# Finishing tokens ahead of the last expert, and half of the first additions on GpSimd

## The chip, the cores and the metric

One core of a Trainium2 chip runs the program; float32 throughout. The time is device microseconds of one execution. Before the change three runs took 1734.29 to 1737.38 us, median 1736.76.

## The reference

One layer of a hybrid decoder on 1024 tokens of width 1024: RMSNorm, a combined projection, a linear-recurrence branch and an attention branch, merged, projected and added to x. Then, and here the change lies, RMSNorm, a mixture of 32 experts and a final RMSNorm:

```python
comb_w = p_group * jax.nn.softmax(top_v, axis=-1)      # a token has two experts, in one group of eight
hb = jax.nn.silu(xb @ w1[e]) * (xb @ w3[e])            # expert e on its tokens: 1024 -> 512
y = hb @ w2[e]                                         # 512 -> 1024
out = x + sum over the token's two experts of w * y
return rms_norm(out, g_final)
```

So a token is finished by: its x, plus low-numbered slot's row times its share, plus high-numbered slot's row times its share, squares summed, root, reciprocal, and the product with g_final.

## The kernel before, in words

Float32 products are made of three products of split operands: ScalarE makes a high part (`piece_hi`, L2032), VectorE the low part (`piece_lo`, L2038, two inputs in SBUF), TensorE multiplies (L2054 for gate and up, L2067 for down). The 1024 tokens are 8 tiles of 128 rows, the residual x2 stays in SBUF.

The last stage (`route_experts`, L2571) first routes (`rest`, L1767): per tile, the last product is added to x2 (`add_rows`), the row is normalized, stored to xn_d, and experts are chosen. Then `experts` (L2070) runs one body per expert. Each expert has 96 slots (BLK); slot rows are gathered from xn_d by an indirect DMA that POOL issues (L2122), one body ahead. Weights come in pieces of 1 MB, six per expert, into a ring of 12 buffers (e_raw), all issued by SP (L2022) in order; a piece waits until TensorE has used the one 12 pieces earlier. An expert's result leaves PSUM by a ScalarE copy (`rows_out`, L2196) and is stored to y_d (`rows_store`, L2200). An expert with more than 96 rows has its surplus in extra blocks behind the 32 (`beyond`, an If on a count from memory, with a loop).

Between the first six bodies VectorE does small chained operations on [128, 8] and [128, 32] tiles (`surplus`, `places`, `destinations`, `blocks`, `row_order`, `shares`, L2403 to L2453): where each token's rows lie and what shares they have. `Steps.did` makes each wait for the one before it. `row_order` stands between bodies 4 and 5, `shares` between 5 and 6.

The end, all programs in order on their engine: POOL, when expert 30's rows are stored, issues eight gathers `EARLY` (L2273) of each token's lower slot row, as far as it lies before expert 31, into tiles `near`, which lie over the piece buffers 0 to 3; a row that lies in expert 31 gets a zero share. VectorE adds each, times its share, to x2 (L2456). When expert 31's rows are stored, POOL issues eight gathers `LATER` of the higher slot row into tiles `far`, over buffers 4 to 7. Per tile VectorE adds, ScalarE squares and sums (L2393) and takes the root (L2395), VectorE takes the reciprocal (L2468) and multiplies (L2472), one and two tiles behind the add; SP stores the tile to out (L2250):

```python
            for t in range(NT):
                dve.wait_ge(near_added, t + 1)
                dve.wait_ge(far_in[t], 16)
                add(far, LATER, t, added)
                if t >= 2:
                    norm(t - 2)
                if t >= 1:
                    root(t - 1)
```

Of the kernel before, what the change touches and what calls it, by code (L numbers as in the profile page):

```python
# [108 lines left out]
class Kernel:  # L109
    def __init__(self, nc, ins, out):  # L110
# [13 lines left out]
        self.slots_d = dram("slots_d", (SLOTS + BLK, 1), I32)  # L124
        self.y_d = dram("y_d", (SLOTS, D))
# [1476 lines left out]
    def project_first(self):  # L1602
# [17 lines left out]
        self.rows_of = high.put("rows_of", [P, 3, NT], I32)  # L1620
        self.share = high.put("share", [P, 3, NT])
# [23 lines left out]
        prod, before_t = put("rt_prod", [P, NT, NE]), put("rt_before_t", [P, NT + 1, NE])  # L1645
        e_base = self.e_base = put("rt_ebase", [P, NT, NE])
# [120 lines left out]
        def rest():  # L1767
# [7 lines left out]
            to_exp, exped = sem("rt_to_exp"), sem("rt_exped")  # L1775

            def sync(sp):
# [246 lines left out]

    def piece_hi(self, act, piece):
# [44 lines left out]
    def experts(self):  # L2070
# [16 lines left out]
        swapped, kept, here, one, two, row = (order.put(f"ls_{n}", [P, NT]) for n in ("swapped", "kept", "here", "one", "two", "row"))  # L2087
# [3 lines left out]
        total, mean, rstd, power = (final.put(f"cb_{n}", [P, NT]) for n in ("total", "mean", "rstd", "power"))  # L2091
        small = final.put("cb_small", [P, 1])
        over = {"near": Map(nc, self.work_start, self.high), "far": Map(nc, self.act_start + 4 * NT * D, self.raw_end)}
        near, far = ([over[n].put(f"cb_{n}{t}", [P, D]) for t in range(NT)] for n in ("near", "far"))
        EARLY, LATER, SURPLUS = range(3)
# [6 lines left out]
        g_in, const, surplus_ready, near_added, surplus_added, added, squared, rooted, powered, normed, out_stored = (  # L2102
            sem("cb_" + n) for n in ("g", "const", "surplus_ready", "near_added", "surplus", "added", "squared", "rooted", "powered", "normed", "stored"))
        ROOT = D ** -0.5

# [119 lines left out]
        def sync(sp):  # L2225
# [21 lines left out]
            beyond(sp, other, before=lambda: sp.wait_ge(near_added, NT))  # L2247
            for t in range(NT):
                sp.wait_ge(normed, t + 1)
                sp.dma_start(k_.out[t * P:(t + 1) * P, :], far[t][:, :]).then_inc(out_stored, 16)  # L2250
            sp.wait_ge(out_stored, 16 * NT)

        def gpsimd(pool):

            for j in range(2, NE):
                gather(pool, j, j % 2, k_.slots_i[0:BLK, j:j + 1])
            pool.wait_ge(dest_out, 2)
# [10 lines left out]
            pool.memset(power[:, :], -0.5).then_inc(const, 1)  # L2268
            pool.memset(small[:, :], EPS).then_inc(const, 1)

            def rows(which, t, to, done):
                upto = BLK * (NE - 1) if which == EARLY else SLOTS
                pool.indirect_dma_start(out=to[t][:, :], out_offset=None, in_=k_.y_d[0:upto, :],  # L2273
                                        in_offset=bass.IndirectOffsetOnAxis(ap=k_.rows_of[:, which, t:t + 1], axis=0))\
                    .then_inc(done[t], 16)

            def all_stored(n):
                pool.wait_ge(y_stored[0], 16 * (NE // 2 + (n + 1) // 2))
                pool.wait_ge(y_stored[1], 16 * (NE // 2 + n // 2))

            def surplus_rows(n):
                pool.wait_ge(const, 2)
                pool.wait_ge(near_added, NT)
                all_stored(n)
                pool.tensor_tensor(total[:, :], power[:, :], power[:, :], ALU.mult).then_inc(surplus_ready, 1)
                pool.wait_ge(surplus_ready, 1)
                for t in range(NT):
                    rows(SURPLUS, t, near, near_in)
# [4 lines left out]
            for t in range(NT):  # L2293
                rows(EARLY, t, near, near_in)
# [102 lines left out]
        def vector(dve):  # L2397
# [125 lines left out]
            for t in range(NT):  # L2523
# [3 lines left out]
                if t >= 2:  # L2527
                    norm(t - 2)
# [68 lines left out]
```

## Time and profile before

| | us |
|---|---|
| three runs | 1734.29, 1736.76, 1737.38 |
| profiled execution, own time | 1740.18 |
| its span, first to last instruction | 1738.5 |
| TensorE busy | 1641.7 (94%) |
| VectorE busy | 1240.6 (71%) |
| ScalarE busy | 898.6 (52%) |
| POOL busy | 132.5 (8%) |

The span is what the trace covers; the profiled execution's own time is 1.7 us longer. A busy share is an average over stages: in the expert stage, from about 1123 us, TensorE and the DMA engines are both busy nearly all the time, in the last 38 us TensorE does nothing. Times inside the trace are from the span's start. DVE is VectorE, ACT ScalarE, POOL GpSimd; a q behind a name is the engine's instruction queue issuing a DMA.

### The profile page before, as it was taken

What the parts mean: (1) busy time and instruction counts of PE and PEld (TensorE: products, weight loads), DVE (VectorE), ACT (ScalarE), POOL (GpSimd) and SP (SyncE); (2) the same over time, 40 slices, a digit from 0 to 9 for tenths busy, and PEclk for the clock granted to TensorE, in tenths of its full rate; (3) what the DMA queues carried; (4) which work ended last, traced back from release to release, by engine and by line L of the source; (5) the groups of instructions that cost most, each with busy time, mean ns of one, the idle gap of its engine ahead of it and who ended that gap; (6) DMA issues with size and microseconds to landing.
All of it is one profiled execution on the core that took longest, in us unless ns stands there. A gap on an engine that the chain in (4) does not pass through costs nothing. (4 is left out here: it accounts for less than half of the span.)

```text
span 1738.5 us, 22942 instructions
## 1 busy us (share of the span) xinstructions
PE 1641.7 (94%) x8288; PEld 1312.9 (76%) x8288; DVE 1240.6 (71%) x1505; ACT 898.6 (52%) x1038; POOL 132.5 (8%) x180
## 2 busy tenths in 40 slices
PE   6999999999999999999989999699999999999991
PEld 6888888888888898778878898566677777777660
DVE  6877776666349882277764426699988888888886
ACT  6343343334237650166642112377777878787773
POOL 1000000000011100022200000100000000000104
PEclk9999999999999999999999999799999999999995
DMA  5354453333255442577662321599999999999988
GB/s 172 88 180 146 159 180 99 103 114 122 97 157 143 131 136 98 205 245 235 240 209 97 144 66 61 208 386 397 399 392 398 389 398 392 398 391 395 397 317 296
DMA packets 187095, 398.97 MB, mean 229 GB/s; under 512 B 16576, under 2 KB 96592, under 8 KB 186000
## 3 DMA queue, kind: packets, MB, share of 16 engines
q1 hardware_dynamic: 172464, 336.96, 53.7%
q0 software_dynamic: 8384, 29.63, 5.8%
q10 hardware_dynamic: 6176, 31.46, 4.8%
q8 instruction: 42, 0.69, 0.2%
q14 instruction: 29, 0.24, 0.0%
HBM read 326.35 MB, written 71.65 MB: 229 GB/s over the span
## 5 line engine op out<-in xcount | busy, mean ns | idle before, releaser
L2038 DVE TENSOR_TENSOR e_l<-e_raw,e_h 128x2048 fp32r<-128x2048 f32 x192 | 439.2, 2290 | 64.4 <-ACT e_h L2032 63.9
L2032 ACT ACTIVATE e_h<-e_raw 128x2048 fp32r<-128x2048 f32 x192 | 368.2, 1919 | 87.5 <-PE ps L2067 44.5
L2054 PE MATMUL ps<-e_h,e_xth 128*96 128x512 f32 x512 | 205.1, 401 | 5.1 <-DVE e_l L2038 3.2
L2054 PE MATMUL ps<-e_h,e_xtl 128*96 128x512 f32 x512 | 202.7, 396 | 0.0
L2054 PE MATMUL ps<-e_l,e_xth 128*96 128x512 f32 x512 | 201.8, 394 | 0.0
L823 DVE TENSOR_TENSOR wn_stl<-wn_stl,ps 128x512 f32<-128x512 f32 x140 | 96.0, 686 | 56.4 <-PE ps L771 49.3
L223 PE MATMUL ps<-uh,w_h 128*128 128x512 f32 x384 | 122.6, 394 | 6.8 <-DVE ul L1340 3.8
L223 PE MATMUL ps<-ul,w_h 128*128 128x512 f32 x384 | 122.2, 393 | 0.0
L223 PE MATMUL ps<-uh,w_l 128*128 128x512 f32 x384 | 122.0, 392 | 0.0
L2054 PEld LDWEIGHTS ps<-e_h,e_xth 128*96 128x96 f32 x512 | 83.0, 162 | 45.2 <-issue 7.4
L2054 PEld LDWEIGHTS ps<-e_h,e_xtl 128*96 128x96 f32 x512 | 83.0, 162 | 36.2
L2054 PEld LDWEIGHTS ps<-e_l,e_xth 128*96 128x96 f32 x512 | 83.4, 163 | 32.2
L795 ACT ACTIVATE wn_stl<-wn_stl 128x512 f32<-128x512 f32 x48 | 30.5, 635 | 133.2 <-DVE wn_stl L823 133.2
L223 PEld LDWEIGHTS ps<-uh,w_h 128*128 128x128 f32 x384 | 72.4, 189 | 23.1 <-DVE ul L1340 4.6
L2067 PE MATMUL ps<-e_h,e_hth 128*96 128x512 f32 x256 | 82.4, 403 | 2.4 <-DVE e_htl L2191 2.4
L223 PEld LDWEIGHTS ps<-ul,w_h 128*128 128x128 f32 x384 | 73.1, 190 | 15.3
L223 PEld LDWEIGHTS ps<-uh,w_l 128*128 128x128 f32 x384 | 72.8, 190 | 15.5
L2067 PE MATMUL ps<-e_l,e_hth 128*96 128x512 f32 x256 | 80.6, 396 | 0.0
L2067 PE MATMUL ps<-e_h,e_htl 128*96 128x512 f32 x256 | 80.3, 395 | 0.0
L2122 POOL DMA_INDIRECT e_xg<-xn_d,slots_i x30 | 43.4, 1446 | 468.4 <-PE ps L2133 468.4
L201 ACT ACTIVATE w_h<-w_raw 128x2048 fp32r<-128x2048 f32 x18 | 34.4, 1913 | 85.2 <-DMA w_raw<-w_lru_out 47.1
L233 PE MATMUL ps<-w_h,uh 128*128 128x256 f32 x256 | 73.6, 288 | 2.1 <-issue 2.1
(695 smaller groups left out, 3649.9 us busy)
## 6 DMA issues: line engine op xcount, KB each, us to landing
e_raw<-w_exp_gate SPq DMA_DIRECT2D x64, 1024.0 KB, 20.9
e_raw<-w_exp_up SPq DMA_DIRECT2D x64, 1024.0 KB, 20.9
e_raw<-w_exp_down SPq DMA_DIRECT2D x64, 1024.0 KB, 20.9
wn_raw<-w_in SPq DMA_DIRECT2D x40, 512.0 KB, 4.8
at_qk<-qk_d ACTq DMA_DIRECT2D x6, 2048.0 KB, 9.3
y_d<-e_y ACTq DMA_DIRECT2D x32, 384.0 KB, 6.5
y_d<-zeros POOLq DMA_DIRECT2D x22, 384.0 KB, 4.6
w_raw<-w_in SPq DMA_DIRECT2D x8, 1024.0 KB, 5.5
```

The source lines that it names most:

```text
L201: act.activation(self.w_h[s][:, :, :], self.w_raw[s][:, :, :], ACT.Copy).then_inc(self.w_hi[s], 1)
L223: mm = pe.matmul(ps[:, h * HALF:(h + 1) * HALF], w[:, k, :], u[:, k, h * HALF:(h + 1) * HALF], start=first, stop=last)
L233: mm = pe.matmul(ps, u[:, k, rows], w[s][:, k, :], start=first, stop=last)
L795: act.activation(result, result, ACT.Gelu_apprx_tanh if HALVED[n][0] == "G" else ACT.Sigmoid).then_inc(final, 1)
L823: dve.tensor_tensor(out, part, bank(n, name), ALU.add).then_inc(added, 1)
L2032: act.activation(self.e_h[m % SPLIT][:, :, :], self.e_raw[slot][:, :, :], ACT.Copy).then_inc(self.e_hi[m % SPLIT], 1)
L2038: dve.tensor_tensor(self.e_l[slot][:, :, :], self.e_raw[slot][:, :, :], self.e_h[m % SPLIT][:, :, :].bitcast(F32), ALU.subtract).then_inc( ...
L2054: mm = pe.matmul(ps, x[:, k, :], w[:, k, :], start=first and first_piece, stop=last and last_piece)
L2067: mm = pe.matmul(ps[:, c * HALF:(c + 1) * HALF], x[:, at, :], w[:, 2 * k + c, :], start=first, stop=last)
L2122: pool.indirect_dma_start(out=xg[b][:, :], out_offset=None, in_=k_.xn_d, in_offset=bass.IndirectOffsetOnAxis(ap=slots, axis=0)).then_inc(g ...
```

## The change

A token none of whose rows is in expert 31 needs nothing of expert 31. After the change all tokens are finished as if there were no expert 31, with clamped indices; the tokens that expert 31 does have are finished a second time, in expert 31's own 96 slots, as a ninth "ending", and their rows scattered to out. In parts:

- Routing: SP stores x2's tiles to DRAM (x2_d) as they are made, eight stores of 0.5 MB.
- `row_order` makes five index lists with every copy waited for; `endings` (after body 5, for `shares`) makes the shares, the scatter index `TO` (a row that expert 31 finishes is sent beyond the last row, where the bounds check drops it), and for expert 31's slots their token and its place in front_d.
- Between gathers 16 and 18 POOL stores front_d (each token's lower row and its two shares) and gathers expert 31's rows of x2_d (last_x) and of front_d (last_of).
- The last expert: `rows_out` and the store of expert 30 go first on ScalarE, `h_low` ahead of the low part of piece 5 on VectorE. Expert 31's rows are neither copied nor stored, unless there is surplus.
- POOL starts the early gathers when down piece 4 of expert 31 has landed, expert 29's rows are stored and the up pieces of expert 30 are used (not: when expert 30's rows are stored). They are clamped below expert 30. Behind them, when expert 30's rows are stored, come the gather of last_y (the lower rows of expert 31's tokens), then the eight later gathers, clamped below expert 31.
- The adds of the lower row to tiles 4 to 7: ScalarE multiplies near by the share, in place, and POOL adds it to x2 (two inputs in SBUF, 128x1024); tiles 0 to 3 stay on VectorE.
- Endings in the order 0, 1, 2, 3, last, 4, 5, 6, 7. The last one adds ps_y from PSUM. Tiles 0 to 3 are stored plainly by SP, the others and the last one scattered by POOL, the last one behind the four plain stores.
- Surplus, if there is any, is handled by finishing everything again (`again`), from x2_d.

```diff
+                def keep(t):
+                    sp.wait_ge(rows_added, t + 1)
+                    sp.dma_start(k_.x2_d[t * P:(t + 1) * P, :], k_.x2[:, t, :]).then_inc(x2_stored, 16)
+                for t in range(NT - 1):
+                    keep(t)
                 sp.wait_ge(rows_mm, NT)
                 for m in range(4):
                     k_.load_piece(sp, (0, 0, m), ("gate", "up")[m // 2], m % 2, 0, True)
+                keep(NT - 1)
...
+        LAST = BLK * (NE - 1)
+        ENDING = (0, 1, 2, 3, NT, 4, 5, 6, 7)
+        PLAIN, BY_POOL = 4, 4
...
             for j in range(2, NE):
                 gather(pool, j, j % 2, k_.slots_i[0:BLK, j:j + 1])
+                if j == NE // 2:
+                    pool.wait_ge(ordered, 7)
+                    pool.dma_start(k_.front_d.rearrange("(p t) a -> p (t a)", p=P), front[:, :, :].rearrange("p t a -> p (t a)"))\
+                        .then_inc(last_in, 16)
+                    pool.wait_ge(k_.x2_stored, 16 * NT)
+                    indexed(last_x[:, :], k_.x2_d, k_.slots_i[0:BLK, NE - 1:NE], last_in)
+                if j == NE // 2 + 1:
+                    pool.wait_ge(last_in, 32)
+                    indexed(last_of[:, :], k_.front_d, last_at[:, 0:1], last_in)
...
-            pool.wait_ge(ordered, 3)
-            pool.wait_ge(y_stored[0], 16 * (NE // 2))
+            k_.piece_in(pool, (NE - 1, 1, 4))
+            pool.wait_ge(y_stored[0], 16 * (NE // 2 - 1))
             pool.wait_ge(y_stored[1], 16 * (NE // 2 - 1))
+            k_.piece_done(pool, (NE - 2, 0, 3))
             for t in range(NT):
                 rows(EARLY, t, near, near_in)
...
+            pool.wait_ge(y_stored[0], 16 * (NE // 2))
+            pool.wait_ge(last_in, 48)
+            indexed(last_y[:, :], k_.y_d[0:LAST, :], last_of[:, 0:1], last_in)
+            for t in range(NT):
+                rows(LATER, t, far, far_in)
+            for t in range(BY_POOL, NT):
+                pool.wait_ge(shared, t + 1 - BY_POOL)
+                pool.tensor_tensor(k_.x2[:, t, :], k_.x2[:, t, :], near[t][:, :], ALU.add).then_inc(front_added, 1)
+
+            def scatter(e, index):
+                _, _, done, _ = rows_of(e)
+                pool.wait_ge(normed, ENDING.index(e) + 1)
+                pool.indirect_dma_start(out=k_.out, out_offset=bass.IndirectOffsetOnAxis(ap=index, axis=0), in_=done,
+                                        in_offset=None, bounds_check=T - 1, oob_is_err=False).then_inc(placed, 16)
+            for e in ENDING[PLAIN + 1:]:
+                scatter(e, row_at[:, TO, e:e + 1])
+                if e == PLAIN:
+                    pool.wait_ge(out_stored, 16 * PLAIN)
+                    scatter(NT, last_to[:, 0:1])
...
+            rows_out(act, j - 1, 0, (j, b, 1))
+            rows_store(act, j - 1, 0)
             k_.piece_hi(act, (j, b, 4))
-            rows_out(act, j - 1, 0, (j, b, 1))
             act_silu(act, j, (j, b, -1))
-            rows_store(act, j - 1, 0)
             k_.piece_hi(act, (j, b, 5))
             h_high(act, j, (j, b, 1))
-            rows_out(act, j, 1, (j, b, 5))
-            rows_store(act, j, 1)
...
+            for t in range(BY_POOL, NT):
+                act.wait_ge(near_in[t], 16)
+                act.activation(near[t][:, :], near[t][:, :], ACT.Copy, scale=share[:, LO, t:t + 1]).then_inc(shared, 1)
...
-            k_.piece_lo(dve, (j, b, 5))
             h_low(dve, j)
-            for t in range(NT):
+            k_.piece_lo(dve, (j, b, 5))
+            for t in range(BY_POOL):
                 dve.wait_ge(near_in[t], 16)
-                add(near, EARLY, t, near_added)
+                add(near, LO, t, early_added)
+            dve.wait_ge(last_in, 64)
+            add_last(last_y[:, :], LO)
+            dve.wait_ge(g_in, 16)
+            for at, e in enumerate(ENDING):
+                if e < NT:
+                    if e < BY_POOL:
+                        dve.wait_ge(early_added, e + 1)
+                    else:
+                        dve.wait_ge(front_added, e + 1 - BY_POOL)
+                    dve.wait_ge(far_in[e], 16)
+                    add(far, HI, e, later_added)
+                else:
+                    k_.piece_done(dve, (NE - 1, 1, 5))
+                    dve.wait_ge(last_added, 1)
+                    add_last(ps_y[:, :], HI)
+                if at >= 2:
+                    norm(ENDING[at - 2], at - 1)
+                if at >= 1:
+                    root(ENDING[at - 1], at)
```

## Rows read from the trace of the kernel before

**Rows 1.** The chain that ended last, in order of time: start us, us, engine, line, count
```profile
1693.01 7.37 PE ps L2067 x24
...
1701.45 5.17 DMA y_d<-e_y
```

**Rows 2.** VectorE's timeline, the tail: start us, us, line, out<-in, count [idle before <-releaser]
```profile
1696.61 1.28 DVE L2456 SCALAR_TENSOR_TENSOR x<-cb_near,share,x 128x1024 f32<-128x1024 f32 x1 [3.66 <-DMA cb_near<-y_d,rows_of]
...
1709.61 1.28 DVE L2456 SCALAR_TENSOR_TENSOR x<-cb_near,share,x 128x1024 f32<-128x1024 f32 x1 [0.46 <-DMA cb_near<-y_d,rows_of]
...
1711.92 1.28 DVE L2456 SCALAR_TENSOR_TENSOR x<-cb_far,share,x 128x1024 f32<-128x1024 f32 x1 [1.02 <-DMA cb_far<-y_d,rows_of]
...
1724.47 1.28 DVE L2456 SCALAR_TENSOR_TENSOR x<-cb_far,share,x 128x1024 f32<-128x1024 f32 x1 [1.08 <-DMA cb_far<-y_d,rows_of]
...
1729.39 1.27 DVE L2456 SCALAR_TENSOR_TENSOR x<-cb_far,share,x 128x1024 f32<-128x1024 f32 x1
...
1733.36 1.29 DVE L2472 SCALAR_TENSOR_TENSOR cb_far<-x,cb_rstd,cb_g 128x1024 f32<-128x1024 f32 x1
```

**Rows 3.** DMA issues of single windows, issue's engine, size, us from issue to landing
```profile
out<-cb_far SPq DMA_DIRECT2D x1, 512.0 KB, 2.6
...
cb_far<-y_d,rows_of POOLq DMA_INDIRECT x1, 4.1
```

**Rows 4.** Stretches: bounds, us, busy of PE PEld DVE ACT POOL, PEclk, DMA share, GB/s
```profile
1259.42:1277.11 17.69, 17.69 (x86) 12.49 (x85) 15.58 (x10) 13.98 (x10) 1.42 (x1) 1.00 1.03 396
...
1648.55:1666.24 17.69, 17.69 (x85) 12.50 (x84) 16.10 (x10) 14.46 (x11) 0.00 (x0) 1.00 1.03 411
```

**Rows 5.** VectorE's timeline between the sixth and the seventh expert
```profile
1242.66 0.16 DVE L2400 TENSOR_TENSOR ls_one<-ls_kept,wgt 128x8 f32<-128x8 f32 x1
...
1244.66 4.50 DVE L2038 TENSOR_TENSOR e_l<-e_raw,e_h 128x2048 fp32r<-128x2048 f32 x2 [0.23 <-DVE share L2453]
```

**Rows 6.** The chain in order of time, products behind row_order and behind shares
```profile
1228.69 3.00 PE ps L2054 x12
...
1247.10 3.00 PE ps L2054 x12
```

**Rows 7.** ScalarE's timeline, a wait for a landing
```profile
1637.93 1.92 ACT L2032 ACTIVATE e_h<-e_raw 128x2048 fp32r<-128x2048 f32 x1 [1.62 <-DMA e_raw<-w_exp_down]
```

**Rows 8.** VectorE's timeline, operations beside gathers on POOL
```profile
1690.20 2.28 DVE L2038 TENSOR_TENSOR e_l<-e_raw,e_h 128x2048 fp32r<-128x2048 f32 x1
...
1698.72 2.64 DVE L2456 SCALAR_TENSOR_TENSOR x<-cb_near,share,x 128x1024 f32<-128x1024 f32 x2 [0.82 <-DMA cb_near<-y_d,rows_of]
```

**Rows 9.** POOL's timeline, gathers of the early and the later rows
```profile
1690.70 2.66 POOL L2273 DMA_INDIRECT cb_near<-y_d,rows_of  x1 [59.23 <-DMA y_d<-e_y]
...
1699.02 1.80 POOL L2273 DMA_INDIRECT cb_near<-y_d,rows_of  x1 [0.30 <-issue]
...
1712.02 1.99 POOL L2273 DMA_INDIRECT cb_far<-y_d,rows_of  x1 [0.30 <-issue]
...
1719.58 0.94 POOL L2273 DMA_INDIRECT cb_far<-y_d,rows_of  x1 [0.30 <-issue]
```

**Rows 10.** ScalarE's queue, and the landing of that store (window 1686 to 1688)
```profile
1686.90 0.33 ACTq L2200 DMA_DIRECT2D y_d<-e_y  x1
...
y_d<-e_y ACTq DMA_DIRECT2D x1, 384.0 KB, 3.0
```

**Rows 11.** SP's queue, and the landing of a down piece (window 1661 to 1664)
```profile
1661.64 5.39 SPq L2022 DMA_DIRECT2D e_raw<-w_exp_down  x2
...
e_raw<-w_exp_down SPq DMA_DIRECT2D x1, 1024.0 KB, 20.6
```

**Rows 12.** POOL's groups by form: busy us, mean ns | idle before
```profile
L1466 POOL TENSOR_TENSOR at_bias<-at_bias,at_mask 128x128 f32<-128x128 f32 x64 | 29.4, 460 | 111.4 <-DVE at_small L1582 98.6 <-DMA at_bias<-bias_d 12.6 <-POOL at_mask L1455 0.3
...
L2301 POOL TENSOR_TENSOR cb_total<-cb_power 128x8 f32<-128x8 f32 x1 | 0.2, 242 | 2.9 <-DMA y_d<-e_y 2.9
```

More of the change, by code:

```diff
@@ L2086, in experts @@
         dst = [order.put(f"ls_dst{s}", [P, NT]) for s in range(2)]
-        swapped, kept, here, one, two, row = (order.put(f"ls_{n}", [P, NT]) for n in ("swapped", "kept", "here", "one", "two", "row"))
+        swapped, kept, one, row = (order.put(f"ls_{n}", [P, NT]) for n in ("swapped", "kept", "one", "row"))
         warm = order.put("e_warm", [1, 2])
@@ L2246, in sync @@
             sp.dma_start(g_b[:, :], k_.ins["g_final"].partition_broadcast(P)).then_inc(g_in, 16)
[L2247 to L2253 removed]
+            for e in range(PLAIN):
+                sp.wait_ge(normed, ENDING.index(e) + 1)
+                sp.dma_start(k_.out[e * P:(e + 1) * P, :], far[e][:, :]).then_inc(out_stored, 16)
@@ new lines, in sync, with indexed, rows, all_stored @@
+            beyond(sp, other, before=all_out, after=again)
+            all_out()
+        def gpsimd(pool):
+            def indexed(to, of, index, done):
+                pool.indirect_dma_start(out=to, out_offset=None, in_=of,
+                                        in_offset=bass.IndirectOffsetOnAxis(ap=index, axis=0)).then_inc(done, 16)
+            def rows(which, t, to, done):
+                upto = {EARLY: LAST - BLK, LATER: LAST}.get(which, SLOTS)
+                indexed(to[t][:, :], k_.y_d[0:upto, :], row_at[:, which, t:t + 1], done[t])
+            def all_stored(n):
+                pool.wait_ge(y_stored[0], 16 * (NE // 2 + (n + 1) // 2))
+                pool.wait_ge(y_stored[1], 16 * (NE // 2 + n // 2))
@@ new lines, in gpsimd, with again @@
+            for e in ENDING[PLAIN + 1:]:
[3 more added lines that the diff above has]
+                    scatter(NT, last_to[:, 0:1])
+            def again(n):
+                all_stored(n)
+                pool.tensor_tensor(spare[:, :], small[:, :], small[:, :], ALU.mult).then_inc(const, 1)
+                pool.wait_ge(const, 2)
+                for t in range(NT):
+                    rows(LOW, t, near, near_in)
+                    rows(HIGH, t, far, far_in)
@@ L2298, in gpsimd @@
+            beyond(pool, lambda j, b, t: gather(pool, j, b, None, t), after=again)
             pool.wait_ge(idx_in[0], 16 * (n // 2 + 1))
             pool.wait_ge(idx_in[1], 16 * ((n + 1) // 2))
-            pool.wait_ge(const, 2)
-            pool.tensor_tensor(total[:, :], power[:, :], power[:, :], ALU.mult).then_inc(const, 1)
-            pool.wait_ge(const, 3)
-            for t in range(NT):
-                rows(LATER, t, far, far_in)
         def tensor(pe):
@@ L2455, in add @@
-            def add(rows, which, t, done):
-                dve.scalar_tensor_tensor(out=k_.x2[:, t, :], in0=rows[t][:, :], scalar=k_.share[:, which, t:t + 1],
-                                         in1=k_.x2[:, t, :], op0=ALU.mult, op1=ALU.add).then_inc(done, 1)
-            def surplus_rows(n):
-                dve.wait_ge(near_added, NT)
-                for t in range(NT):
-                    dve.wait_ge(near_in[t], 32)
-                    add(near, SURPLUS, t, surplus_added)
-                dve.wait_ge(surplus_added, NT)
@@ new lines, in add, with add_last @@
+            def add(of, which, t, done):
+                dve.scalar_tensor_tensor(out=k_.x2[:, t, :], in0=of[t][:, :], scalar=share[:, which, t:t + 1],
+                                         in1=k_.x2[:, t, :], op0=ALU.mult, op1=ALU.add).then_inc(done, 1)
+            def add_last(of, which):
+                dve.scalar_tensor_tensor(out=last_x[:, :], in0=of, scalar=last_of[:, 1 + which:2 + which].bitcast(F32),
+                                         in1=last_x[:, :], op0=ALU.mult, op1=ALU.add).then_inc(last_added, 1)
@@ L2500, in vector @@
             body(5, 1)
-            shares()
+            endings()
             in_pairs(dve, body, 3, NE // 2 - 1)
```

175 lines of the change are left out of this document (106 added, 69 removed).

## The prediction

> **What bounds the kernel now.** I read the page's chain first, then the chain in order of time, then the timelines of VectorE (DVE), POOL and SP behind 1640 us. The chain runs through TensorE for nearly the whole expert stage and leaves it at its end [rows 1]: last down products until 1700.4, store of the last expert's rows (1701.45, 5.17 us), gathers of the later rows, then VectorE. The reader is to see in [rows 2] that VectorE's last stage decides: its first later add starts at 1711.92, its last norm ends at 1734.65 (1733.36 + 1.29). The last store is issued at once and takes 2.6 us [rows 3], so it lands at 1737.3 and the span ends 1.2 us later, at 1738.5. The profiled execution took 1740.18 us against a median of 1736.76; I work out a difference on the span and add it to the median.
>
> **The front of the stage.** The tiles of x that SP now stores (8 of 0.5 MB) go out in the routing stage. Each wait on SP (the add of a tile) ends before the one that SP has anyway (the products of the last tile); only the eighth store stands behind the first four loads, and the next load waits for a gather in any case. Zero; with that cover gone, 0.5 MB at the 396 GB/s of [rows 4] would be 1.3 us.
>
> Between expert bodies VectorE does small chained steps: the nine of shares start at 1242.66, and the next subtraction at 1244.66 after 0.23 us of waiting [rows 5], so 0.20 us each and 0.2 at the end. row_order has ten now, three of them not waited for (0.08): 1.65 us; after, 12 that all wait, 2.4 us. `endings` has 19 steps, 4.0 us, in the place of 2.0. What do they cost? From the products behind row_order (1228.69) to those behind shares (1247.10) the period is 18.41 [rows 6]; in an undisturbed body it is 17.69, all of it TensorE [rows 4]. So of 2.0 us of steps 0.7 reached TensorE and 1.3 was slack. The steps of now have used that slack, so all of the extra, 0.75 + 2.0, reaches it: TensorE is 2.8 us later from the sixth expert on.
>
> It is not lost in full. The loads are as tight as TensorE: ScalarE waits 1.62 us for a landing at 1637.93 [rows 7]. A TensorE that is late lets the loads get ahead. The change gives them work as well: a gather of 96 rows (last_x), the small last_of and the store of front_d. A body with a gather moved 396 GB/s, one without 411 [rows 4]: 17.69 us x 15/411 is 0.65 us; 0.39 MB at 396 is 1.0; 0.4 for the small ones. The loads drain 2.1 us later (bounds 1.0, the bytes alone, and 2.8, TensorE's delay passed on).
>
> **The last expert.** ScalarE's copy of expert 30's rows goes ahead of the high part of piece 4, and VectorE's h_low ahead of the low part of piece 5 (2.28 us from 1690.20 [rows 8]). The down products wait for h_low: about 1 us gained. But nothing on the path waits for them any more: the last expert's own ending reads ps_y as fifth of nine. Worth zero either way. Its rows are no longer stored and gathered: 5.2 us of landing and the wait behind it go.
>
> **When the early gathers start.** Now POOL starts them at 1690.70 [rows 9], 0.8 us after expert 30's rows are stored (1686.90 + 3.0 [rows 10]). After, they wait for expert 29's rows, long stored by then, and for the landing of down piece 4: issued at 1661.64, 20.6 us to landing [rows 11], so 1682.2. With the same 0.8 and 2.1 us of later loads: 1685.1, which is 5.6 us earlier. Eight early gathers lasted from 1690.70 to the add at 1709.61 [rows 2, 9], 18.9 us: the last near tile is there at 1704.0. The rate is seven tiles and one store, 4.06 MB between the adds at 1696.61 and 1709.61, 312 GB/s or 1.7 us a tile. Then last_y (0.39 MB, 1.3 us): 1705.3; far 0 at 1707.0, far 1 at 1708.7, far 2 at 1710.4. POOL's own issuing at the pace of now is 13.4 us for eight, 1.3 for last_y, 12.9 for the eight later ones: it is through at 1712.7.
>
> **VectorE's tail.** The low part of piece 5 is over at about 1696.5; four early adds of 1.28 us and last_y's add end before far 0 is there. Endings 0, 1 and 2 start at 1707.0, 1708.7 and 1710.4; the add of 2 and the first norm end at 1712.9, and from there one add and one norm take 2.46 us (two steps from 1724.47 to 1729.39 [rows 2]). Endings 3 to 8 start at 1712.9, 1715.3, 1717.8, 1720.2, 1722.7 and 1725.1; from the last add's start to the last norm's end it was 5.26 us (1729.39 to 1734.65): 1730.4. Then a scatter from POOL. No scatter is in the trace; bounds are the 2.6 us of an idle plain store and the 5.17 of the store at 1701.45; I take 4.1, the first later gather on an idle queue [rows 3], since it is the same kind of instruction. With 1.2 us behind it the span ends at 1735.7, 2.8 us under now. One ending more (2.46 us) and the scatter (1.5 us) eat most of what the earlier start brings.
>
> **The four adds on GpSimd.** This is the disputed term. An add of 128x128 takes 460 ns there, a product of 128x8 242 [rows 12]: 1.82 ns a column, 2.1 us for 1024; with the second read stream's share unknown I take 2.2. They stand behind POOL's last gather, at 1712.7, when VectorE has no idle time left. If the two engines run beside each other they cost nothing: the first is needed at 1717.8, each next 2.46 us later. But the two get in each other's way. A gather on POOL reads its index from SBUF; it takes 0.94 us when it starts no later than a VectorE operation (1719.58 [rows 9]). The one at 1690.70 took 2.66: VectorE had begun a subtraction at 1690.20 that ended at 1692.48 [rows 8]; 1.78 us of it were left, 1.72 is the extra. The one at 1699.02 began 0.30 us into an add of 1.28 [rows 8]: 0.98 left, 0.86 extra. At 1712.02, 0.10 us into an add: 1.18 left, 1.05 extra. So POOL's read waits for the end of a VectorE operation with two SBUF inputs. The add of a tile and its norm are both of that kind. The other direction, VectorE waiting for POOL, this trace does not show: bounds are 0 and the four adds in full, 4 x 2.2 = 8.8 us. I take the upper side, because these rows look like one door that is held for a whole operation, less what slips by: the last expert's ending reads PSUM and one SBUF input and can run beside a GpSimd add (1.3 us). 7.5 us: VectorE ends at 1737.9, the span at 1743.2, 4.7 us over now.
>
> The Trainium skill (SBUF — State Buffer, section Who interferes with whom) says that a VectorE instruction with two SBUF inputs contends with a GpSimd instruction that reads SBUF; its section SBUF: two separate sides says that whoever starts first has the shared ports for its whole instruction. The rows above agree for POOL's side; by that rule the tail has the 7.5 us, without it it ends at 1735.7. The skill's GPSIMD Engine Reference (Elementwise — side-by-side cycle accounting) gives 4497 ns for 2048 columns, by which an add here is an estimated 2.25 us.
>
> **Rivals.**
> 1. VectorE does not wait for POOL. For it: no VectorE row here is longer for a POOL one, the add at 1711.92 and the norm at 1733.36 are 1.28 and 1.29. Against: no POOL row here reads for long. Then -2.8 us, 1734.0, and 1731 if the loads also drain only 1 us later and the scatter is as quick as a plain store. Not slower. It decides if VectorE's steps keep their 1.28 us beside POOL's four adds.
> 2. The start is late too. The early gathers now fall beside three VectorE subtractions of 2.28 us, each of which can hold one gather up to 1.7 us, where seven of eight had a freer engine; with the exclusion and 0.7 us more of late loads that is up to 4 us more, 1745. Against: the DMA, at 312 GB/s, and not POOL sets the pace.
> 3. The second pass (`again`) runs, if an expert has more than 96 rows. Against: POOL's timeline has 8 gathers into near, not 16, so these data have no surplus. It would add over 20 us: eight more endings at 2.46.
>
> **How the numbers follow.** Forecast, exclusion: 0.48, 1736.76 + 4.7 = 1741.5 (own range 1737.5 to 1746). Rival 1: 0.39, 1734.0 (1730 to 1737). Rival 2: 0.11. Rival 3: 0.02. A measurement of this kernel tells 0.2%, 3.5 us: faster is under 1733.3, slower over 1740.2. Slower: 0.28 of the first, nearly all of rivals 2 and 3, 0.41. Faster: half of rival 1 and a trace of the first, 0.20. Within: 0.39. Cases of both signs hold most of the chance, so the range takes both, 1731 to 1746.
>
> **What would show it.** The small steps: products after the sixth body 2.8 us later. The early start: first near gather at about 1685. The tail: VectorE's adds and norms behind 1712 stretched to 2 us and more, or with gaps before them, beside four POOL adds of 2.1 us or more. If these adds and norms keep 1.28 without gaps, rival 1 is right. The forecast is wrong altogether if VectorE's first later add starts outside 1704 to 1711, or if the last scatter lands over 6 us after the last norm.

## The result, and the profile after

| | us |
|---|---|
| the changed kernel, median of 4 runs | 1750.51 (1748.96 to 1755.27) |
| the kernel before on the same chip, median of 4 | 1737.07 (1734.29 to 1740.18) |
| ratio | 1.0085 [1.0063, 1.0107] |
| profiled execution after, own time | 1755.27, span 1753.7 |

The changed kernel is slower by 0.85%: 13.4 us between the medians, 14.8 by the ratio (10.9 to 18.6 by its interval). Forecast were 4.7 us and a range up to 1746. The profiled execution is the longest of its four, and 3.1 us of it lie ahead of the change's ground: GpSimd's first work of the routing stage starts at 1044.50 where it was 1041.35, and the first gather of the expert stage at 1118.44 where it was 1115.31. Half of that is there already at 988; the other half goes with a granted clock of 0.88 (from 1026 to 1040), which the traces of some kernels below show and others don't. Kernels with the same code up to there start the expert stage anywhere between 1112.0 and 1118.4, so I count it to no part of the change. Traces are therefore compared from that gather on ("stage time"), and sizes of parts also by ratios of medians. In stage time the traced span is 12.1 us longer than before, where 4.7 were forecast.

The stretch that decides is VectorE's tail. First VectorE's timeline after the change (start us, us, engine, line, operation, out<-in, count, [idle before <-releaser]), beside [rows 2]:

```profile
1700.84 4.93 DVE L2547 SCALAR_TENSOR_TENSOR x<-cb_near,share,x 128x1024 f32<-128x1024 f32 x4
1709.82 1.28 DVE L2551 SCALAR_TENSOR_TENSOR cb_last_x<-cb_last_y,cb_last_of,cb_last_x 96x1024 f32<-96x1024 f32 x1 [4.06 <-DMA cb_last_y<-y_d,cb_last_of]
1711.19 2.54 DVE L2547 SCALAR_TENSOR_TENSOR x<-cb_far,share,x 128x1024 f32<-128x1024 f32 x2
1714.10 10.78 DVE L2547 SCALAR_TENSOR_TENSOR x<-cb_far,share,x 128x1024 f32<-128x1024 f32 x1
1724.81 1.27 DVE L2562 SCALAR_TENSOR_TENSOR cb_far<-x,cb_rstd,cb_g 128x1024 f32<-128x1024 f32 x1
...
1742.29 1.28 DVE L2562 SCALAR_TENSOR_TENSOR cb_far<-x,cb_rstd,cb_g 128x1024 f32<-128x1024 f32 x1
```

And POOL's timeline of the same stretch, beside [rows 9]:

```profile
1686.66 1.18 POOL L2293 DMA_INDIRECT cb_near<-y_d,rows_of  x1 [48.80 <-DMA e_raw<-w_exp_down]
1688.15 2.09 POOL L2293 DMA_INDIRECT cb_near<-y_d,rows_of  x1 [0.30 <-issue]
1690.54 2.48 POOL L2293 DMA_INDIRECT cb_near<-y_d,rows_of  x1 [0.30 <-issue]
...
1694.56 2.65 POOL L2293 DMA_INDIRECT cb_near<-y_d,rows_of  x1 [0.30 <-issue]
1697.52 0.94 POOL L2293 DMA_INDIRECT cb_near<-y_d,rows_of  x1 [0.30 <-issue]
1698.76 2.97 POOL L2293 DMA_INDIRECT cb_near<-y_d,rows_of  x1 [0.31 <-issue]
...
1713.59 0.95 POOL L2293 DMA_INDIRECT cb_far<-y_d,rows_of  x1 [0.30 <-issue]
1714.56 9.23 POOL L2341 TENSOR_TENSOR x<-x,cb_near 128x1024 f32<-128x1024 f32 x4
1739.23 2.44 POOL L2346 DMA_INDIRECT out<-cb_far,rows_of  x1 [15.44 <-DVE cb_far L2562]
...
1746.00 0.96 POOL L2346 DMA_INDIRECT out<-cb_far,rows_of  x1 [0.30 <-issue]
```

To be seen: one VectorE add takes 10.78 us where each other takes 1.27, and it ends 1.1 us after POOL's four adds (9.23 us, 2.31 each). It lost 9.5 us. The last norm ends at 1743.57, the span 10.1 us later; before, that was 3.85 us [rows 2, 3]. The DMA issues of the window from 1730 (issue's engine, size, median us to landing) say that the landing itself is not the reason:

```profile
out<-cb_far SPq DMA_DIRECT2D x2, 512.0 KB, 2.6
out<-cb_far,rows_of POOLq DMA_INDIRECT x4, 4.1
```

POOL's five scatters stand in a row, so the last is issued (1746.00) 2.4 us after the last norm; it lands 4.1 us later, at 1750.1, which is 6.5 us behind the last norm; and 3.6 us more pass to the end of the span, where there were 1.2 before.

Earlier, in the chain in order of time (start us, us, engine, line, count), beside [rows 6]:

```profile
1232.69 2.98 PE ps L2066 x12
...
1252.99 4.56 PE ps L2066 x12
```

and the stretches at that place (bounds, us, busy of PE PEld DVE ACT POOL, PEclk, DMA share, GB/s):

```profile
1248.00:1251.00 3.00, 2.55 (x12) 1.46 (x10) 2.39 (x13) 2.68 (x3) 0.00 (x0) 1.00 1.02 324
1251.00:1254.00 3.00, 1.01 (x3) 0.69 (x4) 3.00 (x2) 1.50 (x1) 0.00 (x0) 0.90 1.02 412
1254.00:1257.00 3.00, 3.00 (x9) 2.01 (x8) 3.00 (x3) 0.00 (x0) 0.00 (x0) 0.53 1.03 415
```

The period between the marked products is 20.30 us (18.41 in [rows 6]): 1.9 of the steps, as forecast (2.0). In stage time the second group starts 2.8 us later than before, as forecast too. Behind it stands what was not: TensorE was idle for 2.4 us ahead of 1252.99, the granted clock is then 0.53, mostly the lower level of 1.2 GHz, and the next twelve products take 4.56 us instead of 3.0.

### The profile page after: what moved, and what is told of

Read it like the earlier page. It is cut to its first block and busy times, and to the rows that moved or that the text cites. A ratio compares the mean times of both kernels' runs of the same rounds, so it can differ in the third digit from the quotient of the medians.

```text
span 1753.7 us, 22983 instructions
## 1 busy us (share of the span) xinstructions
PE 1643.0 (94%) x8288; PEld 1314.3 (75%) x8288; DVE 1250.4 (71%) x1517; ACT 901.8 (51%) x1044; POOL 152.0 (9%) x191
```

## The experiments

All times in us; "stage time" as above. Four kernels ran on one chip (kernel before there: median 1736.52), four on another (1739.16), two on a third (1740.42), two on a fourth (1740.11).

The changed kernel itself ran only beside the kernel before of the first table, so it is compared with the others by ratios and by stage time.

**No adds on GpSimd.** `PLAIN, BY_POOL = 4, 4` becomes `4, 8`.

> All four GpSimd adds and ScalarE's scaling for them are gone; VectorE makes all eight early adds. Theory 'held port' (VectorE's add at 1714.10 lasted 10.78 us because POOL's four adds, 9.23 us in a row, had the shared read port): no VectorE operation behind 1700 longer than 1.3 us, end 9 to 10 us earlier, median near 1741. Rival 'late row' (that add waited for its data or for memory, the adds on POOL being a coincidence): the long operation stays, time within 2 us of 1750.5. VectorE's four extra early adds (5 us) fall into its wait for last_y (4 us) and cost 0 to 1 us.

Measured 1740.9, ratio 1.0024 [1.0013, 1.0035], against the changed kernel's 1.0085: the four adds are 0.6%, some 10 us, and the long operation is gone, as "held port" had it. VectorE's first later adds and its last norm:

```profile
1705.86 2.47 DVE L2547 SCALAR_TENSOR_TENSOR x<-cb_far,share,x 128x1024 f32<-128x1024 f32 x2
...
1727.49 1.28 DVE L2562 SCALAR_TENSOR_TENSOR cb_far<-x,cb_rstd,cb_g 128x1024 f32<-128x1024 f32 x1
```

From the first later add to the last norm's end it is 22.9 us, 32.4 in the changed kernel: 9.5 of it is the adds.

**Two adds on GpSimd.** `4, 6`.

> Two adds on GpSimd (tiles 6 and 7) instead of four. Held port: one VectorE operation of about 1.3 + 4.6 us, end 4.7 us earlier than with four, median near 1745.5. Late row: no change.

Measured 1744.82, ratio 1.0051 [1.0038, 1.0065]. Its VectorE and POOL timelines:

```profile
1708.24 6.24 DVE L2547 SCALAR_TENSOR_TENSOR x<-cb_far,share,x 128x1024 f32<-128x1024 f32 x1
```

```profile
1708.74 4.64 POOL L2341 TENSOR_TENSOR x<-x,cb_near 128x1024 f32<-128x1024 f32 x2
```

None, two, four adds: 22.9, 27.8, 32.4 us from first later add to last norm. The price is one per add, 2.4 us; "late row" is out.

**The small steps spread.** The 31 steps of `row_order` and `endings` stand in groups of at most 1.25 us behind bodies 4 to 9, instead of behind 4 and 5:

```diff
-            row_order()
+            between()
             body(5, 1)
-            endings()
-            in_pairs(dve, body, 3, NE // 2 - 1)
+            between()
+            body(6, 0)
...
```

> The 12 steps of row_order and the 19 of endings are spread over the gaps behind bodies 4 to 9, at most six (1.2 us) in a gap; everything else as in the changed kernel. Theory 'slack 1.3 us a body': TensorE is 3.8 us (2.7 of steps more than before, 1.1 of those that before had too) earlier from the tenth body on, and the slow product group behind endings (4.56 us for 12 products) is back at 3.0, 1.5 us more. How much of it reaches the end: if the loads pass TensorE's delay on, 4 to 5 us, median near 1746; if the loads' own drain sets the early gathers, 0 to 1 us, median near 1750.

Measured 1750.92, ratio 1.0076 [1.0051, 1.0102]: no change from 1.0085. The same stretches:

```profile
1251.00:1254.00 3.00, 3.00 (x15) 2.10 (x14) 2.55 (x2) 2.44 (x2) 0.00 (x0) 1.00 1.03 410
1254.00:1257.00 3.00, 3.00 (x20) 2.29 (x19) 2.40 (x3) 2.21 (x3) 1.07 (x1) 1.00 1.01 404
```

TensorE no longer idles there and the clock stays 1.00. The drop goes with the gap: the ten traces with all the steps behind bodies 4 and 5 have 2.4 us of idle TensorE there and 4.5 to 4.6 us for the twelve products behind it, the four others (this kernel, the kernel before, the second hybrid form and the adds alone, both below) have neither. Such an idle stretch is not always followed by a drop, though. At the start of the routing stage TensorE waits 2.30 us for its own queue in the kernel before and in the changed kernel, and the first keeps its full clock (0.39 us a product) while the second drops to the lower level (0.63). The kernel before:

```profile
1033.37 0.47 PE L1810 MATMUL ps<-q_h,mix_h 128*128 128x512 f32 x1 [2.30 <-PEq L186]
1033.67 0.39 PE L1810 MATMUL ps<-q_l,mix_h 128*128 128x512 f32 x1
```

and the changed kernel:

```profile
1034.97 0.77 PE L1818 MATMUL ps<-q_h,mix_h 128*128 128x512 f32 x1 [2.30 <-PEq L188]
1035.54 0.63 PE L1818 MATMUL ps<-q_l,mix_h 128*128 128x512 f32 x1
```

Nothing of the spreading reaches the end, the second of the two outcomes expected: the early gathers start at stage time 568.4, in the changed kernel at 568.2, since they wait for the loads. VectorE's own work in front of the tail ends 1.3 us earlier, and it waits longer for last_y (5.75 us, 4.06 in the changed kernel).

**The last expert's ending third instead of fifth.** `ENDING = (0, 1, NT, 2, 3, 4, 5, 6, 7)`, a single execution.

> The last expert's ending stands third instead of fifth, so its add, which reads PSUM and one SBUF tile, falls beside POOL's adds. Theory 'the second SBUF input is what waits': this add takes 1.3 us beside them, and the next operation with two SBUF inputs is the long one, about 8 us; end about 1.2 us earlier. Rival 'any VectorE operation waits for a GpSimd add': the add from PSUM itself takes over 8 us, end unchanged.

Measured 1748.71, span 1747.1. Its VectorE and POOL timelines:

```profile
1708.72 1.28 DVE L2551 SCALAR_TENSOR_TENSOR cb_last_x<-ps,cb_last_of,cb_last_x 96x1024 f32<-96x1024 f32 x1
1709.92 9.57 DVE L2562 SCALAR_TENSOR_TENSOR cb_far<-x,cb_rstd,cb_g 128x1024 f32<-128x1024 f32 x1
```

```profile
1709.16 9.24 POOL L2341 TENSOR_TENSOR x<-x,cb_near 128x1024 f32<-128x1024 f32 x4
```

An add that reads PSUM and one SBUF input runs in 1.28 us beside POOL's add; the norm behind it, with two inputs in SBUF, ends 1.1 us after POOL's last. So it is the operation's kind that makes VectorE wait (the rival is out), and 1.2 us can be saved by placing the other kind there (31.2 us instead of 32.4 from first later add to last norm).

**Plain stores only.** No adds on GpSimd, and SP stores all eight tiles; the scatters are gone, so the last expert's own rows are not written.

```diff
-            for e in range(PLAIN):
+            for e in range(NT):
...
-            for e in ENDING[PLAIN + 1:]:
-                scatter(e, row_at[:, TO, e:e + 1])
...
```

> All adds on VectorE, and all eight tiles stored plainly by SP; the last expert's own ending is computed but not written, so its tokens stay as if there were no such expert. In the run with all adds on VectorE the last norm ended at 1728.77 and the span at 1738.9, 10.1 us behind it; before the change that was 3.85 us. Theory 'scatters are dear at the end' (2.4 us of a queue on POOL, 4.1 us to landing, 3.6 us behind it): the distance is back at 3.9, the median 6 us lower than 1740.9, near 1735, 2 us under before. Rival 'the memory is the limit' (the tail's 13.7 MB have to go through): the distance stays over 8 us, the median over 1739.

Measured 1738.48, ratio 0.9993 [0.9983, 1.0002], 0.31% under the kernel without GpSimd's adds. The last norm, and the last store of its DMA issues from 1733:

```profile
1732.23 1.28 DVE L2555 SCALAR_TENSOR_TENSOR cb_far<-x,cb_rstd,cb_g 128x1024 f32<-128x1024 f32 x1
```

```profile
out<-cb_far SPq DMA_DIRECT2D x1, 512.0 KB, 3.5
```

From last norm to span end it is 4.8 us, with the scatters 10.1: the scatter ending costs 5.3 us. The store is issued at once (1733.55), lands 3.5 us later, and the span ends 1.2 us behind that, as before; the 3.9 us expected are missed by the landing, which took 2.6 before.

**The early start undone.** No adds on GpSimd, early gathers wait for expert 30's rows as before the change:

```diff
-            k_.piece_in(pool, (NE - 1, 1, 4))
-            pool.wait_ge(y_stored[0], 16 * (NE // 2 - 1))
+            pool.wait_ge(y_stored[0], 16 * (NE // 2))
```

> All adds on VectorE, and the early gathers start as before the change, when expert 30's rows are stored (some 10 us later than at the landing of down piece 4). Theory 'VectorE's work from 1694.8 on is the bound of the tail, gathers have 5 us to spare': 4 to 5 us slower than 1740.9, near 1745. Rival 'the early start is worth what it moves': 9 to 10 us slower, near 1750. Rival 'it is worth nothing': no change.

Measured 1749.53, ratio 1.0057 [1.0040, 1.0075]: against the kernel without GpSimd's adds the start is 8.4 us later in stage time (576.5) and the last norm 5.2 us. The early start is worth about 5 us, as the theory had it, and not what it moves.

**Four tiles finished early, four late, in two forms.** Without GpSimd's adds: only tiles 0 to 3 are finished without the last expert and set right by one scatter in mid-tail; tiles 4 to 7 gather their later rows when expert 31's are stored; all stores plain. The second form also spreads the steps.

```diff
-            for t in range(NT):
+            for t in range(PLAIN):
                 rows(LATER, t, far, far_in)
+            for t in range(PLAIN, NT):
+                indexed(near[t][:, :], k_.y_d[0:LAST, :], front[:, t, 0:1], near_in[t])
+            pool.wait_ge(y_stored[1], 16 * (NE // 2))
+            for t in range(PLAIN, NT):
+                rows(HIGH, t, far, far_in)
+            pool.wait_ge(normed, ENDING.index(NT) + 1)
+            pool.wait_ge(out_stored, 16 * PLAIN)
+            pool.indirect_dma_start(out=k_.out[0:PLAIN * P, :], ..., in_=y_sb[0][:, :], ...)
```

> All adds on VectorE; only tiles 0 to 3 are finished without the last expert and corrected from its slots (one scatter, into rows 0 to 511, in mid-tail); tiles 4 to 7 gather their rows after the last expert's are stored, and are stored plainly by SP. VectorE has the same 33 us of work, so by the theory 'VectorE bounds the tail, and scatters at the end cost 6 us' the last norm ends as in the run with all adds on VectorE and the span 3.9 us behind it: near 1735, 1 to 2 us under before. Rival 'the last expert's rows come too late for tile 4': VectorE waits 2 us or more ahead of the sixth ending, near 1738.

> The same, with the small steps spread over the gaps behind bodies 4 to 9 and the four steps of the scatter index left out. Spreading brought nothing while VectorE waited 4 us for last_y; where VectorE works without a pause from the last low part on, it should bring what it moves that part, 1.6 us: near 1733.5, 3 us under before. Rival 'the loads take it back': no gain over the unspread one.

Measured 1739.54, ratio 1.0001 [0.9991, 1.0011], and 1739.07, ratio 1.0002 [0.9992, 1.0011]. The first later add is at stage time 589.1 and 586.4 (596.6 before), the last norm ends at 619.2 and 616.5 (619.3 before). VectorE, in the first form, waits 1.95 us for the second half, as the rival had it:

```profile
1713.18 1.26 DVE L2539 SCALAR_TENSOR_TENSOR x<-cb_near,share,x 128x1024 f32<-128x1024 f32 x1
1716.39 1.28 DVE L2539 SCALAR_TENSOR_TENSOR x<-cb_far,share,x 128x1024 f32<-128x1024 f32 x1 [1.95 <-DMA cb_far<-y_d,rows_of]
```

The forecasts of 1 to 3 us under the kernel before are missed. In its trace the second form's last norm is 2.7 us earlier in stage time than the first's, but the medians, each good to some 2 us, show no such gain. No version beats the kernel before by more than its interval.

**The adds alone, in the kernel before.** Nothing of the change but this:

```diff
+            for t in range(4, NT):
+                pool.wait_ge(shared, t - 3)
+                pool.tensor_tensor(k_.x2[:, t, :], k_.x2[:, t, :], near[t][:, :], ALU.add).then_inc(pool_added, 1)
```

with ScalarE's copies by the share, and VectorE's early adds of tiles 4 to 7 gone.

> The kernel before, with one part of the change alone: the early adds of tiles 4 to 7 are made by GpSimd behind its last gather (ScalarE multiplies by the share); tokens, stores and order as before. Theory (GpSimd's adds keep the door back to back): four adds in a row, about 9.2 us from 1720.5 on; one VectorE add or norm that starts beside them takes some 10 us, the VectorE wait of 1.1 us for the second last gather disappears in it, and the end is 8 to 9.5 us later than in the kernel before, 1745.5 on a chip where that takes 1737 (ratio 1.005). Rival (the adds only cost in the new order, where scatters and last rows stand behind them; in the old order POOL has nothing left to do and VectorE gains four early adds): within 1.5 us of the kernel before.

Measured 1746.44, ratio 1.0034 [1.0024, 1.0045]; from first later add (1712.37) to last norm (until 1742.14) 29.8 us, 22.7 before: 7.0 for the adds. The cost is there without the rest of the change, but smaller than my theory's 8 to 9.5, and in another pattern. VectorE's and POOL's timelines:

```profile
1717.59 1.28 DVE L2479 SCALAR_TENSOR_TENSOR cb_far<-x,cb_rstd,cb_g 128x1024 f32<-128x1024 f32 x1
...
1718.86 3.29 DVE L2463 SCALAR_TENSOR_TENSOR x<-cb_far,share,x 128x1024 f32<-128x1024 f32 x1
1722.07 3.36 DVE L2479 SCALAR_TENSOR_TENSOR cb_far<-x,cb_rstd,cb_g 128x1024 f32<-128x1024 f32 x1
```

```profile
1717.54 0.95 POOL L2274 DMA_INDIRECT cb_far<-y_d,rows_of  x1 [0.30 <-issue]
1718.50 12.42 POOL L2308 TENSOR_TENSOR x<-x,cb_near 128x1024 f32<-128x1024 f32 x4
```

Here the engines take turns: four VectorE operations of 3.3 us, each 2.0 to 2.1 longer than alone, POOL's adds 12.4 us together. VectorE's delay is 8.2 us in sum; 1.1 of it takes the place of a wait for a late far tile that the kernel before has (1724.47 in [rows 2]), which leaves the 7.0. That POOL's adds always run back to back, as I had it by then, is false. A row that differs is who is inside when POOL's first add arrives: here VectorE's norm of 1717.59, 0.9 us under way; in the changed kernel POOL comes from its last gather (1713.59), and VectorE's add is on record at 1714.10, 0.46 us ahead of POOL's first. That this gather kept VectorE out is not shown: the add of 1709.82 began beside a gather too (POOL's of 1709.49) and took its 1.28 us.

**VectorE inside first.** The changed kernel, with one wait ahead of POOL's adds: `pool.wait_ge(later_added, 3)`.

> The changed kernel, but GpSimd's first add waits for VectorE's later add of tile 2, so it is asked for when VectorE goes straight on with the next operation, a norm. Theory (who holds the shared side when GpSimd's first add arrives sets the pattern: with VectorE in it, the two take turns, as in the kernel before with the adds alone; with GpSimd in it, all adds run in a row): VectorE's next four operations take about 3.3 us each, POOL's four adds 12 us together, and the sum of VectorE's delay is 8.3 us instead of 9.5, so from the first later add to the last norm about 31 us (32.4 in the changed kernel); median within 2 us of it. Rival (the changed order always lets GpSimd's adds run in a row): one VectorE operation of about 10.5 us and POOL's adds 9.2 us.

Measured 1751.12, ratio 1.0060 [1.0041, 1.0079]. VectorE's and POOL's timelines:

```profile
1716.41 1.28 DVE L2563 SCALAR_TENSOR_TENSOR cb_far<-x,cb_rstd,cb_g 128x1024 f32<-128x1024 f32 x1
...
1717.68 3.29 DVE L2548 SCALAR_TENSOR_TENSOR x<-cb_far,share,x 128x1024 f32<-128x1024 f32 x1
1720.89 3.36 DVE L2563 SCALAR_TENSOR_TENSOR cb_far<-x,cb_rstd,cb_g 128x1024 f32<-128x1024 f32 x1
...
1724.25 1.26 DVE L2552 SCALAR_TENSOR_TENSOR cb_last_x<-ps,cb_last_of,cb_last_x 96x1024 f32<-96x1024 f32 x1
1725.43 2.12 DVE L2563 SCALAR_TENSOR_TENSOR cb_far<-x,cb_rstd,cb_g 128x1024 f32<-128x1024 f32 x1
```

```profile
1716.58 13.16 POOL L2342 TENSOR_TENSOR x<-x,cb_near 128x1024 f32<-128x1024 f32 x4 [2.15 <-DVE x L2548]
```

As this theory had it: one wait turns the single operation of 10.8 us into turns. The first later add to the last norm takes 29.9 us, 2.5 less than in the changed kernel, because the last expert's PSUM add now falls beside a POOL add (the norm behind it waits only 0.85), and because a turn costs VectorE 2.0 us where an add in a row costs 2.4: 7.0 us in sum, where 8.3 were expected. The ratio falls from 1.0085 to 1.0060; the intervals overlap, so the medians bear out the sign only weakly.

**One add at a time.** Each POOL add waits for a further later add: `pool.wait_ge(later_added, t - 1)`.

> The changed kernel, but each of GpSimd's four adds waits for a further later add of VectorE (the third, fourth, fifth and sixth), so that they come one at a time. Both theories expect four separate stretches of about 2.3 us taken from VectorE, 8.3 to 9.5 us in sum, and no gain by spreading them: median within 2 us of the changed kernel. Rival (the cost is in the adds being asked for together; one at a time they slip beside ScalarE-bound gaps): under 5 us in sum, median 1745 or less where the changed kernel takes 1750.

Measured 1750.76, ratio 1.0060 [1.0041, 1.0078], again 29.9 us. POOL's timeline:

```profile
1714.52 3.24 POOL L2342 TENSOR_TENSOR x<-x,cb_near 128x1024 f32<-128x1024 f32 x1 [1.00 <-DVE x L2548]
1718.99 3.26 POOL L2342 TENSOR_TENSOR x<-x,cb_near 128x1024 f32<-128x1024 f32 x1 [1.23 <-DVE x L2548]
```

Each is 3.25 us: by the 2.31 of an add in the changed kernel, 0.95 waiting for VectorE and 2.3 working. VectorE loses 7.0 us in sum, again with one turn beside the PSUM add; both theories had 8.3 and more. Spreading them gains nothing against turns; the rival with less than 5 us in sum is out.

How far VectorE is ahead does not decide alone who gets in: 0.17 and 0.23 us were enough for turns in these two kernels, where POOL comes from a wait, and 0.46 to 0.50 were not where it comes straight from a gather (changed kernel, two adds, steps spread).

**Plain stores, but from POOL.** No adds on GpSimd; the last expert's own rows are not written.

```diff
-                scatter(e, row_at[:, TO, e:e + 1])
+                pool.wait_ge(normed, ENDING.index(e) + 1)
+                pool.dma_start(k_.out[e * P:(e + 1) * P, :], far[e][:, :]).then_inc(placed, 16)
```

> All early adds on VectorE, tiles 4 to 7 stored by plain DMAs that POOL issues instead of scatters; the last expert's own rows are not written. It tells what in the 10.1 us behind the last norm belongs to the scatter and what to POOL's queue. Theory (queue: any DMA that POOL issues ends the program late): 3.6 us still pass behind the last landing, 8.5 to 10 us from the last norm to the end of the span, median 1742 to 1744 where the kernel before takes 1739. Rival (scatter: only the indexed store is slow to finish): about 5 us behind the last norm as with SP's stores, median 1738.5.

Measured 1741.42, ratio 1.0007 [0.9993, 1.0021], span 1739.9. The last norm in its VectorE timeline, and the median of its four DMA issues by POOL (window from 1720):

```profile
1730.77 1.28 DVE L2560 SCALAR_TENSOR_TENSOR cb_far<-x,cb_rstd,cb_g 128x1024 f32<-128x1024 f32 x1
```

```profile
out<-cb_far POOLq DMA_DIRECT2D x4, 512.0 KB, 3.2
```

The last one's row in its POOL timeline, and its issue alone (window from 1732.3):

```profile
1732.35 0.53 POOL L2350 DMA_DIRECT2D out<-cb_far  x1 [0.86 <-DVE cb_far L2560]
```

```profile
out<-cb_far POOLq DMA_DIRECT2D x1, 512.0 KB, 3.7
```

From last norm to end 7.85 us: 3.1 more than with SP's stores, 2.3 less than with scatters, and under the 8.5 to 10 expected. Issue and landing (0.3 and 3.7) leave about 3.9 us behind the landing, near the 3.6 behind the last scatter and far from SP's 1.2, so that part of the late end goes with POOL's queue, not with the scatter. The rest of the scatters' 10.1 is that the last one is issued 2.4 us after the last norm and not 0.3. By medians the two endings (1.0007, and 0.9993 with SP) can't be told apart. Why the end comes later behind POOL's DMAs no run here shows.

## Why the prediction was wrong

The direction was right (slower, to which I had given 0.41), and VectorE does wait for GpSimd's adds, the disputed term; but the time fell outside the range, and the step that failed most is the ending behind the last norm. The prediction's own sign for that came: it was to be wrong altogether if the last scatter landed over 6 us after the last norm, and it landed 6.5 after it. (The other, VectorE's first later add outside 1704 to 1711, is at 1711.19, and at 1708.1 without the 3.1 us of the stage's start.) In the span, forecast 1743.2 and traced 1753.7, the 10.5 us are: 3.1 of the stage's start, 1.1 of the early gathers, 2.0 of the exclusion, 0.5 less in the rest of the tail, and 4.8 of the ending.

1. *"I take 4.1 ... With 1.2 us behind it"*: the term that failed most. The landing measured 4.1, as taken. But five scatters stand in POOL's queue (the first takes 2.44 us, beside an add and the norm right behind it, the others follow 1.3 to 1.4 apart), so the last is issued 2.4 us late, and the end of the program stands 3.6 us behind the landing. 5.3 forecast, 10.1 measured; replacing the scatters gives 5.3 back. I had costed one scatter on an empty queue, against the prediction's own example of gathers held by VectorE [rows 9] (here even past the end of one operation into the next), and had carried the 1.2 of an SP store over to another engine.
2. *"bounds are 0 and the four adds in full, 4 x 2.2 = 8.8 us ... 7.5 us"*: exclusion is confirmed (rival 1, at 0.39, falls by its own sign: an add of 1.28 us took 10.78 beside them, and with none on GpSimd the ratio is 1.0024). An add took 2.31, the estimate from the Trainium skill's GPSIMD Engine Reference, section Elementwise — side-by-side cycle accounting, was 2.25. In the changed kernel 9.5 us went, above my upper bound: nothing slipped by, as VectorE's add, on record 0.46 us ahead of POOL's first, did not get in until the fourth had ended. Where they take turns it is 8.2 us, or 7.0 with the last expert's PSUM add beside one of them, which is the forecast's own sum, near its 7.5. The Trainium skill (SBUF — State Buffer, SBUF: two separate sides) has the side held for one instruction; the kernels with turns agree (3.3 = 2.0 waiting + 1.3), while the changed kernel's trace shows it held across four.
3. *"Eight early gathers lasted ... 18.9 us: the last near tile is there at 1704.0"*: failed. They start at stage time 568.2, 7.2 us earlier than before (forecast 5.6: 1.6 better). Down piece 4 landed 1.0 us later in stage time (19.7 us behind its issue at 1666.65), my lower bound, where 2.1 were forecast, and POOL went on 0.3 us behind the landing, not 0.8. But from the first gather to the landing of the last near tile it is 21.9 us (ScalarE's copy of it starts at 1708.53), 3.0 more. POOL's issuing took 16.3 us for eight, 13.4 before; the extra is in the gathers that began beside a subtraction (2.09, 2.48, 2.65, 2.97). That is rival 2's mechanism and most of its price (up to 4 us, 0.7 of it for late loads, which did not come). "the DMA, at 312 GB/s, and not POOL sets the pace" does not hold here: the DMA engines are less busy beside these gathers than they were. The ten us from 1695.7 on, before and after (bounds, us, busy of PE PEld DVE ACT POOL, PEclk, DMA share, GB/s):

```profile
1695.70:1705.70 10.00, 4.66 (x18) 2.92 (x16) 6.35 (x5) 2.51 (x3) 6.84 (x6) 0.84 0.98 331
```

```profile
1695.70:1705.70 10.00, 6.83 (x31) 4.19 (x29) 8.84 (x8) 5.50 (x7) 8.23 (x6) 1.00 0.85 289
```

   The last tile lands 5.6 us behind POOL's last issue, 5.5 before and 4.9 in the kernel with the late start, so the landing moves with POOL's issuing (16.3, 13.4 and 14.8 us). The first gathers also share the DMA engines with the last loads now (7.8 and 8.0 us to the landing of the second and third, 5.7 to 7.1 before); what that adds no run splits off. The first later add is 3.9 us earlier than before, 4.9 forecast; last_y's 1.3 us were as forecast; the 1.4 behind it, 1.7 in the forecast, are VectorE's own add of last_y and not a wait for the first far tile.
4. *The small steps*: 1.9 us in the period and 2.8 in all, as costed; the lower clock behind it, 1.5 us more, was missing. Neither reaches the end of the changed kernel: with the steps spread the early gathers start no sooner (568.4).
5. *The x2 stores at zero*: right. From POOL's first work of the routing stage to the stage's first gather it is 73.9 to 74.0 us in every trace, before and after.
6. *"One ending more (2.46 us) and the scatter (1.5 us) eat most of what the earlier start brings"*: right in kind. With plain stores and no GpSimd adds the earlier start (worth 5 us) pays for the ninth ending and gives the time of before, 0.9993. Nothing is left that could pay for the scatters or the adds.

Of the 14.8 us by the ratio, some 10 are GpSimd's adds (1.0085 to 1.0024) and 5 the scatters (to 0.9993). The terms that the forecast had too small are the ending (by 4.8 us) and the adds (by 2.0).

## What to carry to other kernels

Before moving elementwise work to GpSimd, look at what VectorE runs then: if it has two inputs in SBUF and no idle time, each GpSimd operation costs VectorE about its whole length (2.0 to 2.4 us here for 128x1024), and no more than a PSUM operation's 1.2 us, or a wait that was there anyway, hid any of it. Cost a new ending by its engine's whole queue and by what passes from the last landing to the end, not by one transfer: POOL's scatters ended the program 10.1 us after the last result, SP's stores 4.8. Finishing most of the data ahead of the last piece gained 5 us, and with plain stores and no GpSimd adds the kernel stood where it had been: what the last piece's own ending brought with it cost about as much. No run splits that cost.

## What the runs showed of the hardware that was not expected

- The same four GpSimd adds cost VectorE 9.5 us in one operation of 10.8, or 8.2 in four turns of 3.3 (7.0 with a PSUM operation in one of them); one wait ahead of the adds moved it from the one to the other. Why a waiting VectorE is passed over four times in one case and never in the other stays open.
- POOL is passed over too: issuing a gather takes 0.94 us, and took 3.22 (1705.92, the kernel without its adds) beside two VectorE adds that follow each other, longer than the rest of the first alone would make it.
- 2.4 us of idle TensorE were followed by a granted clock of 0.53 and 1.5 us lost in all ten traces that have them at the sixth expert; 2.30 us of it at the routing stage were followed by the lower level in the changed kernel and by the full clock in the kernel before.
- 3.6 us (scatters) and about 3.9 us (plain) pass from the landing of POOL's last DMA to the end of the span, 1.2 with SP's.
